# Down products of a four-tile group issued between the pairs of the next group, part of the low-part work moved to VectorE, squares of the norms moved to ScalarE

## The chip, the cores and the metric

One core of a Trainium2 chip runs one program. The metric is the device time of that program in microseconds, the median of the timed runs. The kernel before was run three times.

## The reference

One hybrid decoder layer over 512 tokens with 16 learned meta tokens in front (528 tokens, model width 1024, float32):

```
h = concat(meta, x)
h = h + 0.5 * swiglu(rmsnorm(h, ffn1_norm), w_gate, w_up, w_down)      # d_ff 2816: FFN 1
h = h + concat(gla(hn), sparse_attention(hn)) @ w_out                  # the mixer
h = h + 0.5 * swiglu(rmsnorm(h, ffn2_norm), w_gate, w_up, w_down)      # FFN 2
out = rmsnorm(h, final_norm)[16:]
```

with `swiglu(h) = (silu(h @ w_gate) * (h @ w_up)) @ w_down`. The change touches the two FFNs and the norms that follow them; the mixer between them keeps its instructions.

## The kernel before

All activations lie transposed, feature on the partitions and tokens along the row: h is 8 tiles of 128 x 528. In FFN 1 a product runs over 2 x 264 tokens; in FFN 2 the meta tokens are dropped, so it is 512 (or 2 x 256).

**Three-term products.** Every float32 operand is split into a high part (a copy rounded to fp32r, made on ScalarE) and a low part (operand minus high part, a subtraction). A product is three matmul streams: high by high, high by low, low by high. For the weights the high part is `hi`, `hi_w`, `hi_s` (ACT, L1814 to L1832), and the low part is `lo`, `lo_pair` (POOL, L1704 to L1719).

**Tiles and groups.** The 22 tiles of 128 hidden features are in `GROUPS = [(0, 4), (4, 6), (10, 6), (16, 6)]`. Group 0 is plain: gate and up product of each tile, then silu and the product. Groups 1 to 3 work on two tiles at once with a seven-product scheme (Strassen-Winograd): one *pair* unit is the gate (or the up) weights of two tiles, and is computed in 7 products of half width, each 4 k-steps x 3 streams = 12 matmuls, 84 in all (`pair`, L2235). Even m is a gate pair, odd m an up pair, and two such iterations give two tiles. A pair needs four sums of weight quarters (`sums`, DVE, L2018 to L2023, four operations of 128x512), and its seven products are combined by seven additions on DVE (L2120 to L2134). The low parts of a pair are four POOL operations, in all seven quarters: w11 and w12 (L1711, 1024 wide), w22 (L1714, 512 wide), s2 and s1, and s3 and s4 (L1719, 1024 wide each). After an up pair, DVE multiplies (L2131, L2138), ACT makes the high part `ah` (L1856) and DVE the low part `al` (L2034).

**Down products.** Once a whole group is through, `down` makes the 8 output tiles d, each over all the tiles of the group (L2203), in a ring of four bank pairs; DVE adds each into h (`add_down`, L2056). So TensorE runs 6 pairs in a row, then 8 down products in a row.

**What orders the work.** There is no planner: each engine has its own program, written out in order, with semaphore counts between them. On VectorE, an iteration of a pair is: sums of the next pair, low part of the tiles before, the additions, the multiplications. `w_split` counts weight low parts, `w_used` counts finished products (which free a place of the weights), `c_add` the additions (which free the PSUM banks of a pair), `h_done` the additions into h. Raw weights come through a ring of four slots (`raw`), loaded by SP in the order of use; a load waits until the low part of the unit four before it is made.

**After an FFN.** While the last group's down products run, DVE does for each d: `add_down` (L2056), the square (L1987), the sum of squares (L1990) and, before the mixer, the low part of the mixer's input (L1996); ACT makes its high part (`prep_hi`, L1842). The mixer's first product waits for these low parts one by one. After FFN 2 ACT scales h instead (L1940).

**Plain group.** DVE makes the x operands of the seven-product scheme beside the plain tiles: xn (L2080), their low parts (L2039), and four sums of quarters `x_sums` (L2045 to L2050), all four between the third and the fourth plain tile.

Of the kernel before, what the change touches and what calls it, by code (L numbers as in the profile page):

```python
# [51 lines left out]
GROUPS = [(0, 4), (4, 6), (10, 6), (16, 6)]  # L52
PLAIN = GROUPS[0][1]
FFN_UNITS = 2 * FT + KT * len(GROUPS)
# [18 lines left out]

HALF_UNIT = UNIT // 2
DOWN_PLACES = [0, 2, 4, 6, 8, 10, 12, 8]
PLACE, Q_END, Q_FREE, WIDTH = {}, {}, {}, {}
PAIR_N, PAIRS_OF = {}, {}


def lay_out():  # L80
    taken, q = [0] * 14, 0

    def put(u, place, size, units, width=UNIT):
        nonlocal q
        free, q = max(taken[place:place + size]), q + size
        taken[place:place + size] = [q] * size
        for v in range(u, u + units):
            PLACE[v], Q_END[v], Q_FREE[v], WIDTH[v] = place, q, free, width

    def put_ffn(u, base):  # L90
        for g, (f0, cnt) in enumerate(GROUPS):
            if g == 0:
                for v in range(u, u + 2 * cnt):
                    put(v, 2 * ((v - base) % RING), 2, 1)
            else:
                for n in range(cnt):
                    PAIR_N[u + 2 * n] = len(PAIR_N)
                    put(u + 2 * n, 7 * (n % 2), 7, 2)
            u += 2 * cnt
            for d in range(KT):  # L100
                put(u + d, DOWN_PLACES[d], 2, 1, cnt * P)
            u += KT

    put_ffn(U_FFN1, U_FFN1)
    for u in range(U_MIX, U_FFN2):
        put(u, 2 * ((u - U_MIX) % RING), 2, 1)
    put_ffn(U_FFN2, U_MIX)


lay_out()  # L110

# [6 lines left out]

# [55 lines left out]
def build(nc, x, meta, ffn1, ffn2, mix_norm, w_in, w_a2, b_a, head_norm, w_out, final_norm,  # L174
          cos_t, sin_t, out):
    ctx = ExitStack()
    with ctx:
# [46 lines left out]
        wxh = sb("wxh", [P, 3, UNIT], F32R, ffn_scope)  # L224
        wx_scope = ExitStack()
        wxl = sb("wxl", [P, 3, UNIT], F32R, wx_scope)
        wx_scope.close()
        wxs = sb("wxs", [P, 3, UNIT], F32, ffn_scope)
# [82 lines left out]
        def seven_bank(g, m, i):  # L311

            return (2 * (g - 1) + 7 * m + i) % 8

        def down_bank(g, d):
            return 2 * ((d + g) % 4)
# [3 lines left out]
        w_split = sem("w_split")  # L320
# [643 lines left out]
        def act_mixer(act, hi, prep_hi, root):  # L964
            def keep_part(bank, dst, u, parts):
                ((_, t, n),) = parts
                act.wait_ge(w_used, Q_END[u])
                act.activation(dst[:, t:t + n], ps[:, bank, 0:n], ACT.Copy).then_inc(pj_kept, 1)

            def keep(bank, dst, rows, u, i=None):  # L970
                act.wait_ge(w_used, Q_END[u])
                act.activation(halves(dst), ps[0:rows, bank:bank + 2, 0:HALF], ACT.Copy).then_inc(pj_kept, 1)

            def keep_v(dst, m0, blocks, cols, first):

                act.wait_ge(w_used, Q_END[U_MIX + m0 + 3])
# [213 lines left out]
        def dve_mixer(dve, prep, prep_lo):  # L1190
# [34 lines left out]
            dve.wait_ge(w_used, Q_END[U_MIX + M_IKW])  # L1225
# [22 lines left out]
            dve.wait_ge(w_used, Q_END[U_MIX + M_GV + 3])  # L1248
# [104 lines left out]
            def keep_fill(m):  # L1353

                unit = M_GQK + m
                dve.wait_ge(w_used, Q_END[U_MIX + unit])
# [141 lines left out]
            def add_early(d):  # L1498
                dve.wait_ge(w_used, Q_END[U_OUT + (d - 4) // 2])
# [48 lines left out]
            def add_out(d):  # L1548
                if d % 2 == 0:
                    dve.wait_ge(out_even, d // 2 + 1)  # L1550
                else:
                    dve.wait_ge(w_used, Q_END[U_OUT + 4 + d // 2])
# [24 lines left out]
        def _(sp):  # L1577
            def load(u, src, dst_view):

                slot = u % RING  # L1580
                if u >= RING:
                    sp.wait_ge(w_split, Q_END[u - RING])
                sp.dma_start(dst_view(raw[:, slot, :]), src).then_inc(w_in_slot[slot], 16)
# [19 lines left out]
            def ffn_loads(weights, u0):  # L1603
# [4 lines left out]
                u = u0  # L1608
                for g, (f0, cnt) in enumerate(GROUPS):
                    tiles = range(f0, f0 + cnt)  # L1610
                    if g == 0:
                        order = [(v, f) for f in tiles for v in (gate_v, up_v)]
                    else:
                        order = [(v, f + j) for f in tiles[::2] for v in (gate_v, up_v) for j in range(2)]
                    for v, f in order:
                        load(u, v[:, :, f * P:(f + 1) * P], cols())
                        u += 1
                    for d in range(KT):
                        load(u, down_v[:, f0:f0 + cnt, d * P:(d + 1) * P],
                             lambda s: s[:, 0:cnt * P].rearrange("p (k n) -> p k n", k=cnt))  # L1620
                        u += 1

            ffn_loads(ffn1, U_FFN1)
# [60 lines left out]
            ffn_loads(ffn2, U_FFN2)  # L1684
# [9 lines left out]
        def _(pool):  # L1694
# [6 lines left out]
            def lo(u):  # L1701
                n = WIDTH[u]
                pool.wait_ge(w_hi, Q_END[u])
                pool.tensor_tensor(places(1, PLACE[u], 2)[:, 0:n], raw[:, u % RING, 0:n],  # L1704
                                   places(0, PLACE[u], 2)[:, 0:n].bitcast(F32), ALU.subtract).then_inc(w_split, 2)

            def lo_pair(u):

                at_p, q = operand_places(u), Q_END[u] - 7
# [3 lines left out]
                pool.wait_ge(w_hi, q + 3)  # L1713
                pool.tensor_tensor(places(1, at_p["w22"], 1), raw[:, (u + 1) % RING, HALF_UNIT:UNIT],  # L1714
                                   places(0, at_p["w22"], 1).bitcast(F32), ALU.subtract).then_inc(w_split, 1)
                pool.wait_ge(s_done, 4 * (PAIR_N[u] + 1))
                for n, name in enumerate(("s2", "s3")):
                    pool.wait_ge(w_hi, q + 5 + 2 * n)
                    pool.tensor_tensor(places(1, at_p[name], 2), places(2, at_p[name], 2), places(0, at_p[name], 2).bitcast(F32),  # L1719
                                       ALU.subtract).then_inc(w_split, 2)  # L1720

            def ffn(u, first):

                for g, (_, cnt) in enumerate(GROUPS):
# [44 lines left out]
            ffn(U_FFN1, 1 + len(LEVELS))  # L1769
# [32 lines left out]
            ffn(U_FFN2, 0)  # L1802
# [3 lines left out]
        def _(act):  # L1806
            def hi(u):
                slot, n = u % RING, WIDTH[u]
# [5 lines left out]
                act.activation(places(0, PLACE[u], 2)[:, 0:n], raw[:, slot, 0:n], ACT.Copy).then_inc(w_hi, 2)  # L1814
# [34 lines left out]
            def ffn(u0, number, norm):  # L1849
# [29 lines left out]
                act.wait_ge(w_used, Q_END[u - 1])  # L1879
# [509 lines left out]
```

## Time and profile before

| what | us |
|---|---|
| median of 3 runs | 1109.05 (1108.9 to 1109.67) |
| profiled execution, its own time | 1111.36 |
| its span, first to last instruction | 1109.6 |
| TensorE busy | 1051.8 (95%) |
| VectorE busy | 831.0 (75%) |
| GpSimd (POOL) busy | 635.4 (57%) |
| ScalarE busy | 452.6 (41%) |
| mean granted TensorE clock | 0.99 |

The span is 1.76 us shorter than the execution's own time. Busy shares are means over stages with different limits: in the pair stages three engines are nearly full at once, in the mixer they are not.

### The profile page before, as it was taken

What the parts mean: (1) busy time and instruction counts of PE and PEld (TensorE: products, weight loads), DVE (VectorE), ACT (ScalarE), POOL (GpSimd) and SP (SyncE); (2) the same over time, 40 slices, a digit from 0 to 9 for tenths busy, and PEclk for the clock granted to TensorE, in tenths of its full rate; (3) what the DMA queues carried; (4) which work ended last, traced back from release to release, by engine and by line L of the source; (5) the groups of instructions that cost most, each with busy time, mean ns of one, the idle gap of its engine ahead of it and who ended that gap; (6) DMA issues with size and microseconds to landing.
All of it is one profiled execution on the core that took longest, in us unless ns stands there. A gap on an engine that the chain in (4) does not pass through costs nothing.

```text
span 1109.6 us, 18931 instructions
## 1 busy us (share of the span) xinstructions
PE 1051.8 (95%) x7399; PEld 944.3 (85%) x7399; DVE 831.0 (75%) x1210; ACT 452.6 (41%) x688; POOL 635.4 (57%) x329
## 2 busy tenths in 40 slices
PE   6989999999998999999999999999998999899897
PEld 5989989989998998789767777877888899889886
DVE  5889974895499678699776595578898389649955
ACT  5444342443244344462355516433344234414433
POOL 3657874887488545069710203333888388758750
PEclk8999999999999999999999999999999999999999
DMA  6123433234232534434311102221422432334231
GB/s 193 58 69 104 110 102 94 76 86 125 71 100 68 143 99 112 106 96 125 93 52 39 58 1 77 77 58 38 131 79 78 133 95 77 101 89 115 67 86 76
DMA packets 171740, 98.65 MB, mean 89 GB/s; under 512 B 6275, under 2 KB 167094, under 8 KB 171654
## 3 DMA queue, kind: packets, MB, share of 16 engines
q1 hardware_dynamic: 171654, 97.47, 31.3%
q8 instruction: 59, 0.97, 0.4%
q14 instruction: 27, 0.22, 0.1%
HBM read 91.18 MB, written 2.10 MB: 84 GB/s over the span
## 4 chain that ended last, share of the span: by engine, by line
PE 62%; DVE 21%; issue 8%; POOL 5%; ACT 3%; DMA 1%; SPq 0%; DVEq 0%; POOLq 0%; ACTq 0%
PE ps L2203 35%; PE ps L2235 12%; PE ps L500 5%; PE ps L514 4%; DVE wxs L2018 3%; DVE ws L2019 3%; DVE wxs L2019 2%; DVE ws L2018 2%; POOL wxl L1719 2%; DVE ws L2021 2%; POOL wl L1704 1%; PE ps L637 1%; PE ps L681 1%; PE ps L660 1%; DVE wxs L2021 1%
## 5 line engine op out<-in xcount | busy, mean ns | idle before, releaser
L1704 POOL TENSOR_TENSOR wl<-raw,wh 128x1024 fp32r<-128x1024 f32 (+2 forms) x85 | 187.8, 2219 | 300.7 <-ACT wh L1814 261.7
L2203 PE MATMUL ps<-xh,wh 128*128 128x264 f32 (+3 forms) x416 | 122.8, 342 | 7.1 <-DVE xl L1996 5.8
L2056 DVE SCALAR_TENSOR_TENSOR h<-ps,h 128x528 f32<-128x528 f32 (+1 forms) x64 | 43.8, 695 | 104.2 <-PE ps L2203 104.1
L2203 PE MATMUL ps<-xl,wh 128*128 128x264 f32 (+3 forms) x416 | 117.8, 330 | 0.0
L2203 PE MATMUL ps<-xh,wl 128*128 128x264 f32 (+3 forms) x416 | 117.4, 330 | 0.0
L1719 POOL TENSOR_TENSOR wxl<-wxs,wxh 128x1024 fp32r<-128x1024 f32 x36 | 92.0, 2575 | 36.2 <-ACT wxh L1832 33.5
L2235 PE MATMUL ps<-xh,wh 128*128 128x264 f32 (+1 forms) x360 | 103.6, 288 | 7.3 <-POOL wl L1719 7.2
L1704 POOL TENSOR_TENSOR wxl<-raw,wxh 128x768 fp32r<-128x768 f32 (+1 forms) x32 | 60.3, 1903 | 83.5 <-ACT wxh L1814 83.5
L1719 POOL TENSOR_TENSOR wl<-ws,wh 128x1024 fp32r<-128x1024 f32 x36 | 91.2, 2555 | 22.8 <-ACT wh L1832 18.7
L2235 PE MATMUL ps<-xl,wh 128*128 128x264 f32 (+1 forms) x360 | 101.7, 282 | 0.0
L2235 PE MATMUL ps<-xh,wl 128*128 128x264 f32 (+1 forms) x360 | 101.5, 282 | 0.0
L1814 ACT ACTIVATE wh<-raw 128x1024 fp32r<-128x1024 f32 (+2 forms) x85 | 79.3, 950 | 47.3 <-issue 18.5
L2203 PEld LDWEIGHTS ps<-xh,wh 128*128 128x128 f32 (+1 forms) x416 | 71.2, 191 | 23.9 <-issue 15.9
L2235 PE MATMUL ps<-xh,wxh 128*128 128x264 f32 (+1 forms) x216 | 63.9, 296 | 21.6 <-POOL wxl L1719 21.5
L2203 PE MATMUL ps<-ah,wh 128*128 128x264 f32 (+1 forms) x264 | 72.1, 327 | 5.5 <-DVE al L2034 2.8
L2235 PEld LDWEIGHTS ps<-xh,wh 128*128 128x128 f32 x360 | 67.7, 188 | 10.4 <-POOL wl L1719 10.4
L2203 PEld LDWEIGHTS ps<-xh,wl 128*128 128x128 f32 (+1 forms) x416 | 71.2, 191 | 6.3
L2203 PEld LDWEIGHTS ps<-xl,wh 128*128 128x128 f32 (+1 forms) x416 | 71.2, 190 | 4.8 <-issue 0.2
L2203 PE MATMUL ps<-ah,wl 128*128 128x264 f32 (+1 forms) x264 | 71.7, 326 | 0.0
L2203 PE MATMUL ps<-al,wh 128*128 128x264 f32 (+1 forms) x264 | 71.5, 325 | 0.0
L2203 PE MATMUL ps<-ah,wxh 128*128 128x264 f32 (+1 forms) x264 | 70.5, 321 | 0.0
L2203 PE MATMUL ps<-ah,wxl 128*128 128x264 f32 (+1 forms) x264 | 70.5, 321 | 0.0
(292 smaller groups left out, 3223.7 us busy)
## 6 DMA issues: line engine op xcount, KB each, us to landing
raw<-in_ffn_w_gate SPq DMA_DIRECT2D x44, 512.0 KB, 4.2
raw<-in_ffn_w_up SPq DMA_DIRECT2D x44, 512.0 KB, 4.1
raw<-in_ffn_w_down SPq DMA_DIRECT2D x48, 384.0 KB, 3.9
raw<-in_w_in SPq DMA_DIRECT2D x28, 512.0 KB, 4.0
raw<-in_ffn_w_down SPq DMA_DIRECT2D x16, 256.0 KB, 2.8
raw<-in_w_out SPq DMA_DIRECT2D x8, 512.0 KB, 3.4
xin<-in_x SPq DMA_DIRECT2D x4, 512.0 KB, 4.8
out<-xin SPq DMA_DIRECT2D x4, 512.0 KB, 3.6
```

The lines of the kernel that those rows point to most:

```text
L500: mm = pe.matmul(ps[0:n, V_BANKS[m0][b], :], xx[:, 2 * q + k, s:s + n], ww[:, slot, k * 512:(k + 1) * 512], start=(q == 0 and k == 0 and c ...
L514: return pe.matmul(ps[:, bank, :], ww[:, slot, k * 256 + dd * P:k * 256 + (dd + 1) * P], rr[:, tile, META:TOK], start=(starts and k == 0 a ...
L637: pe.matmul(ps[0:w, qk_bank(n), 0:main_keys(b)], pjb[e:e + HD, pair, s:s + w], pjb[e:e + HD, 4 + pair, 0:main_keys(b)], start=True, stop=T ...
L1704: pool.tensor_tensor(places(1, PLACE[u], 2)[:, 0:n], raw[:, u % RING, 0:n], places(0, PLACE[u], 2)[:, 0:n].bitcast(F32), ALU.subtract).the ...
L1719: pool.tensor_tensor(places(1, at_p[name], 2), places(2, at_p[name], 2), places(0, at_p[name], 2).bitcast(F32), ALU.subtract).then_inc(w_s ...
L1814: act.activation(places(0, PLACE[u], 2)[:, 0:n], raw[:, slot, 0:n], ACT.Copy).then_inc(w_hi, 2)
L2018: dve.tensor_tensor(s1, w21, w22, ALU.add).then_inc(s_done, 1)
L2019: dve.tensor_tensor(s3, w11, w21, ALU.subtract).then_inc(s_done, 1)
L2021: dve.tensor_tensor(s2, s1, w11, ALU.subtract).then_inc(s_done, 1)
L2056: dve.scalar_tensor_tensor(out=as_parts(h[:, d, tk], norm), in0=psum_parts(bank, norm), scalar=0.5, in1=as_parts(h[:, d, tk], norm), op0=A ...
L2203: mm = pe.matmul(ps[0:m, bank + a, 0:width], places(lo, PLACE[u], 2)[:, k * P:k * P + m], r[:, tile, t:t + width], start=(k == first and n ...
L2235: mm = pe.matmul(ps[:, seven_bank(g, m, i), 0:w], places(lo, at_p[wn], 1)[:, k * P:(k + 1) * P], x_operand(xlo, xn, w)[:, k, :], start=(k ...
```

## The change

Four edits, in both FFNs.

1. Groups are now 4 plain tiles, 2, and four times 4. Down products of group g are no longer a stage of their own. They run inside the pairs of group g+1: in each pair, one down product after its third product and one after its seventh. Group 0's down products still run in a row, and so do the last group's. There are six groups of down products instead of four (so 48 additions into h in each FFN instead of 32), over the same 22 tiles: TensorE's matmuls are the same in number and size. A pair uses banks 0 to 5, the down products between use banks 6 and 7 only, so each waits for the addition of the one before. Weight places go from 14 to 16 half units; down weights of four tiles take one place.
2. The low parts of w22 and of s3 and s4 (three of seven) go from POOL to VectorE (`low_pair`), which makes them for the next pair between its second and third addition.
3. After an FFN, ACT squares h (`square`) behind `prep_hi`, and DVE only adds the squares up.
4. Two of the four `x_sums` move behind the fourth plain tile.

```diff
-GROUPS = [(0, 4), (4, 6), (10, 6), (16, 6)]
+GROUPS = [(0, 4), (4, 2), (6, 4), (10, 4), (14, 4), (18, 4)]
+A_TILE = [0, 4, 0, 4, 0, 4]
...
+            def low_pair(u):
+                at_p, n, q = operand_places(u), PAIR_N[u], Q_HI[u] - 7
+                dve.wait_ge(w_hi, q + 3)
+                dve.tensor_tensor(places(1, at_p["w22"], 1), raw[:, (u + 1) % RING, HALF_UNIT:UNIT],
+                                  places(0, at_p["w22"], 1).bitcast(F32), ALU.subtract).then_inc(w_split_dve, 1)
+                dve.wait_ge(w_hi, q + 7)
+                dve.wait_ge(s_done, 4 * (n + 1))
+                dve.tensor_tensor(places(1, at_p["s3"], 2), places(2, at_p["s3"], 2), places(0, at_p["s3"], 2).bitcast(F32),
+                                  ALU.subtract).then_inc(w_split_dve, 2)
...
                     # VectorE, one iteration (g, m); "after" is the next pair
+                    if after:
+                        sums(U_PAIR[(number, *after)])
+                    dve.wait_ge(p1_kept, n + 1)
+                    ...two additions...
+                    if after:
+                        low_pair(U_PAIR[(number, *after)])
+                    if g > 1:
+                        add_down(g - 1, 2 * m)
+                    ...the other additions, and after an up pair the multiplications and low()...
+                    if g > 1:
+                        add_down(g - 1, 2 * m + 1)
+                for d in range(KT):
+                    add_down(last, d)
+                    prep(norm + 1, d)
+                    if number == 0:
+                        prep_lo(norm + 1, d)
...
                     # TensorE
+                def step_down(g, d):
+                    v = U_DOWN[number, g, d]
+                    pe.wait_ge(w_split, Q_END[v])
+                    pe.wait_ge(h_done, hd + KT * g + d)
+                    down(v, 6, order[g], norm, 0, GROUPS[g][1], ft + GROUPS[g][0] if d == 0 else None)
...
+                        for i, (wn, xn_) in enumerate(SEVEN):
+                            if i == DOWN_AFTER and g > 1:
+                                step_down(g - 1, 2 * m)
+                            if i < 2:
+                                pe.wait_ge(w_split, Q_END[v] - 4 + 2 * (i + 1))
+                            elif i == 2:
+                                pe.wait_ge(w_split_dve, 3 * (n + 1))
...
+                        if g > 1:
+                            step_down(g - 1, 2 * m + 1)
...
                     # ScalarE, after an FFN
+                    square(norm + 1, d, hd + d)
...
                     # SP: a load into a slot that held a pair's weights
+                for v in (u - RING, u - RING - 1):
+                    if v in PAIR_N:
+                        sp.wait_ge(w_split_dve, 3 * PAIR_N[v] + 1)
```

## Rows read from the trace of the kernel before

**Rows 1.** The page: busy time of each engine, share, instructions

```profile
PE 1051.8 (95%) x7399; PEld 944.3 (85%) x7399; DVE 831.0 (75%) x1210; ACT 452.6 (41%) x688; POOL 635.4 (57%) x329
```

**Rows 2.** TensorE's waits: waiter, releaser, total us, times, longest

```profile
PE ps L2235 <- POOL wxl L1719: 21.5, 26, 1.1
PE ps L2235 <- POOL wl L1719: 7.2, 9, 1.1
PE ps L2203 <- DVE al L2034: 2.8, 1, 2.8
...
PE ps L2203 <- POOL wl L1704: 2.7, 1, 2.7
```

**Rows 3.** Windows: length, busy us (count) of PE, PEld, DVE, ACT, POOL; clock, DMA, GB/s

```profile
97.80:165.61 67.81, 62.61 (x501) 60.98 (x500) 60.87 (x71) 27.58 (x40) 56.26 (x24) 1.00 0.36 99
165.61:200.67 35.06, 35.06 (x291) 35.06 (x290) 14.74 (x15) 8.46 (x11) 18.48 (x9) 1.00 0.29 82
200.67:267.35 66.68, 62.55 (x507) 61.48 (x506) 58.12 (x71) 28.27 (x40) 53.68 (x23) 1.00 0.36 100
...
898.45:964.76 66.31, 61.57 (x505) 60.15 (x505) 57.96 (x71) 28.09 (x40) 54.10 (x24) 1.00 0.36 100
```

**Rows 4.** Chain that ended last: start us, us, what, matmuls

```profile
302.41 32.04 PE ps L2235 x264
...
369.05 39.43 PE ps L2203 x312
...
772.73 24.09 PE ps L2203 x96
...
865.02 33.43 PE ps L2203 x144
898.45 9.98 PE ps L2235 x84
```

**Rows 5.** Timeline of VectorE: start us, us, operation [idle before]

```profile
67.79 1.24 DVE L2045 TENSOR_TENSOR xn<-xn 128x1056 f32<-128x1056 f32 x1
...
88.27 0.67 DVE L2018 TENSOR_TENSOR ws<-raw 128x512 f32<-128x512 f32 x1
88.87 0.68 DVE L2019 TENSOR_TENSOR ws<-raw 128x512 f32<-128x512 f32 x1
...
100.43 2.88 DVE L2019 TENSOR_TENSOR wxs<-raw 128x512 f32<-128x512 f32 x1
...
106.10 0.43 DVE L2122 TENSOR_TENSOR t<-ps,t 128x264 f32<-128x264 f32 x1
106.45 0.42 DVE L2123 TENSOR_TENSOR t<-ps,t 128x264 f32<-128x264 f32 x1
```

**Rows 6.** Timeline of POOL: the second and last with VectorE out of its way

```profile
99.92 2.84 POOL L1711 TENSOR_TENSOR wxl<-raw,wxh 128x1024 fp32r<-128x1024 f32 x1
...
76.04 2.54 POOL L1704 TENSOR_TENSOR wl<-raw,wh 128x512 fp32r<-128x512 f32 x2 [10.46 <-ACT wh L1814]
...
410.12 2.39 POOL L1704 TENSOR_TENSOR wl<-raw,wh 128x1024 fp32r<-128x1024 f32 x1 [0.86 <-ACT wh L1814]
```

**Rows 7.** Timeline after FFN 1: VectorE's cycle of one d, and ScalarE

```profile
381.07 0.69 DVE L2056 SCALAR_TENSOR_TENSOR h<-ps,h 128x528 f32<-128x528 f32 x1
381.80 0.71 DVE L1987 TENSOR_TENSOR t<-h 128x528 f32<-128x528 f32 x1
382.54 0.71 DVE L1990 TENSOR_TENSOR ss<-ss,t 128x528 f32<-128x528 f32 x1
383.17 0.76 DVE L1996 SCALAR_TENSOR_TENSOR xl<-h,vecs,xh 128x528 fp32r<-128x528 f32 x1
...
401.15 1.05 ACT L1814 ACTIVATE wh<-raw 128x1024 fp32r<-128x1024 f32 x1
404.89 0.74 ACT L1842 ACTIVATE xh<-h,vecs 128x528 fp32r<-128x528 f32 x1 [2.70 <-DVE h L2056]
```

**Rows 8.** Squares on ScalarE at the start, a table load, the clock after a stall

```profile
29.31 0.65 ACT L1961 ACTIVATE t<-h 128x528 f32<-128x528 f32 x1 [0.20 <-DVE ss L2172]
...
31.87 1.28 ACT L1847 ACT_TABLE_LOAD   x1
...
74.00:80.00 6.00, 3.75 (x22) 3.75 (x23) 3.98 (x4) 5.26 (x8) 3.51 (x3) 0.81 0.17 50
```

More of the change, by code:

```diff
@@ new lines, in ffn @@
+                for d in range(3, KT - 1):
+                    hi(U_DOWN[number, last, d])
+                for d in range(KT):
+                    if d == 1:
+                        hi(U_DOWN[number, last, KT - 1])
+                    if number == 0:
+                        if d >= 6:
+                            hi(U_MIX + d - 6)
+                        prep_hi(1, d, hd + d)
+                    square(norm + 1, d, hd + d)
+                    if number:
+                        act.activation(h[:, d, tk], h[:, d, tk], ACT.Copy, scale=gains[:, 3, d:d + 1]).then_inc(y_done, 1)
@@ L1945, in _, with square @@
+            def square(norm, d, h_count):
+                act.wait_ge(h_done, h_count + 1)
+                if d >= 2:
+                    act.wait_ge(ss_done, norm * KT + d - 1)
+                tk = tokens_of(norm)
+                act.activation(t01[:, d % 2, tk], h[:, d, tk], ACT.Square).then_inc(sq_done, 1)
             act.wait_ge(scrap_done, 1)
@@ L2085, in ffn @@
                             x_low(name)
[L2086 to L2087 removed]
+                        x_sums(True)
+                x_sums(False)
                 x_low("t2")
@@ L2155, in _ @@
+                for d in range(KT):
+                    add_down(last, d)
+                    prep(norm + 1, d)
+                    if number == 0:
+                        prep_lo(norm + 1, d)
             for n in range(0, 10, 2):
@@ new lines, in ffn @@
+                for k0, k1, ds in ((0, PLAIN - 1, range(2)), (PLAIN - 1, PLAIN, range(2)), (0, PLAIN, range(2, KT))):
+                    for d in ds:
+                        v = U_DOWN[number, 0, d]
+                        if k0 == 0:
+                            pe.wait_ge(w_split, Q_END[v])
+                            if d < 4:
+                                pe.wait_ge(up_scaled, PLAIN * (number + 1) - 1 + d // 2)
+                            else:
+                                pe.wait_ge(h_done, hd + d - 3)
+                        down(v, down_bank(0, d), tiles, norm, k0, k1, ft if d == 0 else None)
@@ new lines, in ffn @@
+                cnt = GROUPS[last][1]
+                for k0, k1, ds in ((0, 2, range(3)), (2, cnt, range(3)), (0, cnt, range(3, KT))):
+                    for d in ds:
+                        v = U_DOWN[number, last, d]
+                        if k0 == 0:
+                            pe.wait_ge(w_split, Q_END[v])
+                            if 1 <= d < 4:
+                                pe.wait_ge(c_add, 7 * (n + 1))
+                            else:
+                                pe.wait_ge(h_done, hd + KT * last + (d - 3 if d else 0))
+                        down(v, down_bank(last, d), order[last], norm, k0, k1, ft + GROUPS[last][0] if d == 0 else None)
```

495 lines of the change are left out of this document (222 added, 273 removed).

## The prediction

> **What bounds the kernel now.** I read the page's engine shares first: TensorE is busy 1051.8 of 1109.6 us [rows 1], so at most 58 us can be won without removing matmuls, and the change removes none. Then TensorE's own waits: 35 waits for POOL in the pairs, 28.7 us together, each about 1.1 us, and two single waits of 2.8 and 2.7 us around the plain group [rows 2]. Then windows cut at the stage borders, to see where it waits: the down stage of 165.61 to 200.67 is full (35.06 of 35.06 us), with POOL at 18.48 and VectorE at 14.74; the pair stages are not, and there POOL (54 to 56 us of 67) and VectorE (58 to 61 us) are nearly full [rows 3]. So the kernel alternates a stage in which the helpers are the limit with one in which they idle.
>
> How much the pair stages lose: 264 matmuls took 32.04 us, so a pair of 84 takes 10.2 us in FFN 1, and 9.98 us in FFN 2 [rows 4]. Six are 61.2 and 59.9. FFN 1: the first stage starts at the end of the down products, about 97.0, and ends at 165.61, 68.6 us; the other two last 66.7. Lost: 7.4 + 5.5 + 5.4 = 18.3. FFN 2: from 796.8 (772.73 + 24.09) to 865.02 is 68.2, then twice 66.3 [rows 3, 4]: 8.3 + 6.4 + 6.4 = 21.1. Together 39.4 us, and this is what the change can reach, plus the two single waits.
>
> **Why the helpers are slow.** A 128x512 operation of VectorE with both inputs in SBUF starts 0.60 us after the one before when POOL rests, and takes 2.88 us when POOL works; operations that read PSUM keep 0.43 us, 0.35 apart, beside a busy POOL [rows 5]. POOL's 1024-wide operation takes 2.39 us alone and 2.84 against VectorE, the 512-wide one 1.27 alone [rows 6]. The 2.88 us look like one POOL operation plus the own time.
>
> The Trainium skill (SBUF — State Buffer, Who interferes with whom) says that the two engines share a port pair, which one instruction holds whole while the other blocks. By that, each POOL operation delays at most one VectorE operation, by POOL's own duration; the trace agrees (0.60 + 2.39 is close to 2.88). Read as a rate instead, VectorE would run at a quarter of its speed for POOL's 8.7 us of a pair: 8.7 + (5.5 - 2.2) + 3.75 = 15.8 us against the lock's 16.6, both worked out from the terms of the next part. The lock speaks against the change: the low parts moved to VectorE are two more operations that can each be held.
>
> **Part 1 and 2, the steady pairs (groups 3 to 5, 12 pairs in each FFN).** TensorE needs 10.2 + 2 x 24 matmuls at 35.06/288 = 0.122, so 10.2 + 5.8 = 16.0 us for a pair [rows 3, 4]; in FFN 2 9.98 + 2 x 2.79 (33.43/12) = 15.6. POOL per pair: two 1024-wide and two 512-wide, 2 x 2.39 + 2 x 1.27 = 7.3 us: far from full. VectorE alone: sums 4 x 0.60, low parts 0.60 + 1.17, on average one multiplication 0.7 and one `al` 0.65, in all 5.5 us in SBUF; seven additions at 0.35 and two `add_down` at 0.65, 3.75 us from PSUM [rows 5, 7]: 9.3 us. If every POOL operation delays it in full: 9.3 + 7.3 = 16.6. So both engines fit into TensorE's 16 us on average, VectorE just so at worst, and POOL no longer ends last. What is late next is the second down product: it waits for `add_down` of the first, which VectorE does behind sums, two additions and `low_pair`. TensorE asks for it 13.1 us into the pair (3 products 4.4, down 2.9, 4 products 5.8). VectorE starts its iteration 0.7 us in (behind the last `add_down`), sums 2.4 to 6.1, additions 0.7, low parts 1.8 to 5.4, `add_down` 0.65: done between 6.3 and 13.6 us. After an up pair it starts later by the multiplications, the wait for ACT's high part and `al`, some 2 us: up to 15.6. The stall is so 0 to 0.5 us in every other pair and 0 to 2.5 in the rest; I take 0.33 per pair, nearer the low end because POOL's operations are seldom all in the way: 4 us in each FFN (0 to 18).
>
> **Group 2 (4 pairs).** Its downs belong to the group of two tiles, so TensorE has 10.2 + 2.9 = 13.1 us per pair while VectorE still has 9.3 alone, 15.6 with POOL in the way, and about 1.4 of waits for the last down and for ACT. I take 1.25 us per pair, between 0 and 3.9: 5 us in each FFN. **Group 1 (2 pairs, no downs):** the first is made ready beside the plain downs. The first `al` of it is wanted 4.4 us into the next pair: 1 us (0 to 3). Together the pair stages lose 10 us in each FFN, 20 in all, against 39.4.
>
> The new queue order on SP, POOL and ACT I cost at nothing: loads of a pair now wait for VectorE's w22 part, about 10 us into an iteration, and land some 4 to 5 us later, before the sums of the next iteration at 16.7; in group 2 that cover is 13 us, and up to 1 us per pair is in the upper bound above.
>
> **Part 3, behind FFN 1.** Before, VectorE's cycle for one d is 0.73 + 0.74 + 0.63 + 0.68 = 2.8 us under six-tile downs of 4.38 [rows 3, 7]. Now downs take 2.92, and VectorE must wait for ACT: `add_down` 0.73, `prep_hi` 0.65 (its distance to a next operation), square 0.65 and two hand-overs of 0.04 [rows 7, 8], sum 0.63, low part 0.68: 3.4 us. The chain of eight is then longer than TensorE's. From the end of the last pair: down of the group before 2.9, its `add_down` (the last down row begins in its banks) 0.8, two tiles of three downs 4.4, the first finished at 9.6; eight cycles end at 9.6 + 27.4 = 37, and POOL's interference adds about 1. The mixer's first product needs the last low part and ends at 38.5. Without waits it would be 2.9 + 23.4 + 4.4 = 30.7 (before, 39.43 for both with no stall [rows 4]). Loss 8 us (5 to 10). At a stall of 2.8 us the clock was granted at 0.81 in the 6 us around it [rows 8]; two such stalls here, so 1.5 us more. 9.5 in all. Should Square need another table behind Silu, a load of 1.28 us comes on top [rows 8]; squares ran without one at the start, I take 0. Behind FFN 2 the cycle is 0.7 + 0.7 + 0.65 = 2.1 us under 2.79: hidden, and the end of the chain stays the same (a square on ACT for one on VectorE). Only the bank wait stays, 1 us.
>
> **Part 4 and the places, plain group.** The wait for `al` (2.8) goes since two `x_sums` (2.4 us [rows 5]) are out of the way, the wait for `wl` (2.7) since the first down no longer needs a place of the last plain unit. But the same VectorE work then delays the fifth and sixth down, which want its `add_down`: I estimate that 1.3 of 2.8 and 2.2 of 2.7 remain as a gain, 3.5 us (0 to 6).
>
> **Sum.** -39.4 + 20 + 9.5 + 1 - 3.5 = -12.4. Against the profiled execution, 1111.4 - 12.4 = 1099.0; that ran 2.3 us above the median, so 1096.7, and I say 1096.
>
> **Rivals.** (a) *The helpers are fully covered.* For it: both averages lie under 16 us. Pair stages lose 3 us in each FFN and the tail 7: -39.4 + 6 + 8 - 3.5 = -29, 1080. Against it: the single pair of banks for downs. Chance 0.2. (b) *VectorE becomes the bound, slower than before.* Its place is `add_down` behind sums and `low_pair` in one in-order queue. It has 16.6 us at worst against 16.0, and 15.6 against 13.1. It decides once the pairs of groups 2 to 5 lose 1 us each on average (32 pairs: 32 us). At 1.5 us: 50 + 10.5 - 39.4 - 3.5 = +18, 1127. Chance 0.12. (c) *Given back.* The pairs win as forecast, but the chain behind FFN 1 and the plain group cost 10 us more than I say (a table load, a lower clock, late loads): 1106. Chance 0.13. Forecast: 0.55, its own range 1088 to 1104.
>
> **Range and chances.** 1079 to 1112. A change under 0.2% (2.2 us) can't be told from none. Faster 0.8, same 0.07, slower 0.13.
>
> **What would show it.** TensorE's waits for POOL in the pairs are gone; waits for VectorE's h (second down) or its low parts stand there, under 0.5 us per pair in groups 3 to 5 and about 1 in group 2. POOL is well under 60% busy in the pair stages, VectorE over 80%. Between the last pair of FFN 1 and the mixer TensorE waits 6 to 9 us for xl. I am wrong if the steady pairs come out at 17 us or more, or if the tail does not stall.

## The result, and the profile after

| kernel | median us | runs | ratio to before, 95% interval |
|---|---|---|---|
| before | 1109.17 | 1108.9 to 1109.67 | 1 |
| after | 1126.88 | 1126.08 to 1128.01 | 1.016 [1.0142, 1.0177] |

The change costs 17.7 us. The forecast was 1096, and the time lies outside its range; rival (b) gave 1127. The profiled execution of after took 1126.08 (span 1124.4), 0.8 below its median, that of before 1111.36, 2.2 above, so the traces differ by 14.8 us in span.

The page of after answers to [rows 1]:

```profile
PE 1054.5 (94%) x7399; PEld 949.0 (84%) x7399; DVE 922.0 (82%) x1298; ACT 461.3 (41%) x736; POOL 503.3 (45%) x289
```

POOL has lost 132 us of busy time, VectorE has gained 91, and TensorE has the same 7399 matmuls. TensorE's waits, in the columns of [rows 2]:

```profile
PE ps L2253 <- DVE h L2108: 31.9, 26, 4.4
PE ps L2253 <- issue: 8.0, 3, 6.4
...
PE ps L2253 <- DVE xl L2034: 4.1, 1, 4.1
PE ps L2253 <- POOL wxl L1749: 3.6, 2, 1.9
PE ps L2253 <- DVE al L2083: 2.3, 3, 1.0
```

The 35 waits for POOL in the pairs are gone, as said. In their place stand 26 waits of a down product (L2253) for the addition of the one before it (L2108), 31.9 us in all; 23 of them, 28.7 us, lie in the pairs of groups 2 to 5, the other three in the plain groups' down products. The same by stage, in the columns of [rows 3]: FFN 1's group 1, group 2, groups 3 to 5; FFN 2's group 2 and groups 3 to 5; and six microseconds behind one stall:

```profile
95.02:116.45 21.43, 20.61 (x170) 20.43 (x169) 21.29 (x25) 8.05 (x12) 10.03 (x4) 1.00 0.22 62
116.45:180.54 64.09, 56.02 (x435) 55.29 (x434) 60.68 (x73) 22.87 (x36) 30.47 (x18) 0.95 0.38 102
180.54:381.62 201.08, 196.25 (x1586) 194.37 (x1584) 179.91 (x203) 72.93 (x110) 97.30 (x49) 0.99 0.34 92
827.86:891.98 64.12, 54.17 (x387) 51.00 (x385) 60.68 (x74) 22.96 (x37) 30.83 (x18) 0.96 0.39 105
891.98:1089.05 197.07, 189.46 (x1297) 174.64 (x1295) 178.11 (x201) 71.85 (x110) 97.27 (x48) 1.00 0.34 92
133.40:139.40 6.00, 6.00 (x27) 6.00 (x28) 4.53 (x8) 2.88 (x6) 2.15 (x2) 0.51 0.63 170
```

In group 2 and in groups 3 to 5 POOL is busy for half of the time and VectorE for 95% and 90%; TensorE waits while VectorE still has idle time. How that comes about is in one iteration of VectorE in FFN 2 (timeline, the columns of [rows 5]):

```profile
959.73 0.68 DVE L2108 SCALAR_TENSOR_TENSOR h<-ps,h 128x512 f32<-128x512 f32 x1
960.33 1.20 DVE L2056 TENSOR_TENSOR wxs<-raw 128x512 f32<-128x512 f32 x1
961.46 2.88 DVE L2057 TENSOR_TENSOR wxs<-raw 128x512 f32<-128x512 f32 x1
...
966.37 2.84 DVE L2067 TENSOR_TENSOR wl<-raw,wh 128x512 fp32r<-128x512 f32 x1
969.14 2.31 DVE L2071 TENSOR_TENSOR wxl<-wxs,wxh 128x1024 fp32r<-128x1024 f32 x1
971.37 0.68 DVE L2108 SCALAR_TENSOR_TENSOR h<-ps,h 128x512 f32<-128x512 f32 x1
...
975.26 0.69 DVE L2108 SCALAR_TENSOR_TENSOR h<-ps,h 128x512 f32<-128x512 f32 x1 [1.56 <-PE ps L2253]
```

POOL in the same stretch:

```profile
959.69 1.30 POOL L1749 TENSOR_TENSOR wxl<-raw,wxh 128x512 fp32r<-128x512 f32 x1 [6.06 <-ACT wxh L1857]
960.95 2.84 POOL L1756 TENSOR_TENSOR wxl<-raw,wxh 128x1024 fp32r<-128x1024 f32 x1
...
966.26 2.41 POOL L1761 TENSOR_TENSOR wxl<-wxs,wxh 128x1024 fp32r<-128x1024 f32 x1 [2.47 <-ACT wxh L1875]
968.63 1.74 POOL L1749 TENSOR_TENSOR wxl<-raw,wxh 128x512 fp32r<-128x512 f32 x1
```

And TensorE's down product that waits for it, and one in group 2 of FFN 1:

```profile
972.20 0.47 PE L2253 MATMUL ps<-ah,wxh 128*128 128x512 f32 x1 [0.98 <-DVE h L2108]
...
133.40 0.78 PE L2253 MATMUL ps<-ah,wxh 128*128 128x264 f32 x2 [4.22 <-DVE h L2108]
```

The additions of two successive down products stand at 959.73 and 971.37, 11.6 us apart. Four POOL operations ran between, and each held one VectorE operation: 1.20, 2.88, 2.84 and 2.31 us for operations that take 0.60, 0.60, 0.60 and 1.17 alone. TensorE had waited 0.98 us. Then VectorE, through with its additions, idles 1.56 us for the down product that it had made late itself. TensorE waits for VectorE and VectorE for TensorE by turns, so neither is full: one period of two pairs takes 32.87 us (from 958.3 to 991.2 in TensorE's timeline) where TensorE needs 31.1.

The 2.88 and 2.84 us are again near 0.60 plus a whole POOL operation of 2.39 [rows 6]. By the Trainium skill (SBUF — State Buffer, Who interferes with whom) one instruction holds the port pair of the two engines whole; the trace agrees.

### The profile page after: what moved, and what is told of

Same layout as the page of the kernel before. It is cut to its first block and busy times, and to the rows that moved or that the text cites. A ratio compares the mean times of both kernels' runs of the same rounds, so it can differ in the third digit from the quotient of the medians.

```text
span 1124.4 us, 19157 instructions
## 1 busy us (share of the span) xinstructions
PE 1054.5 (94%) x7399; PEld 949.0 (84%) x7399; DVE 922.0 (82%) x1298; ACT 461.3 (41%) x736; POOL 503.3 (45%) x289
## 5 line engine op out<-in xcount | busy, mean ns | idle before, releaser
L1749 POOL TENSOR_TENSOR wl<-raw,wh 128x1024 fp32r<-128x1024 f32 (+1 forms) x65 | 147.5, 2281 | 270.1 <-ACT wh L1857 232.2
L1749 POOL TENSOR_TENSOR wxl<-raw,wxh 128x512 fp32r<-128x512 f32 (+1 forms) x84 | 128.4, 1532 | 223.9 <-ACT wxh L1857 223.9
L2253 PE MATMUL ps<-ah,wxh 128*128 128x264 f32 (+1 forms) x456 | 126.4, 332 | 37.8 <-DVE h L2108 31.9
L2253 PE MATMUL ps<-xh,wh 128*128 128x264 f32 (+3 forms) x416 | 123.3, 343 | 12.3 <-issue 6.4
L2253 PE MATMUL ps<-ah,wxl 128*128 128x264 f32 (+1 forms) x456 | 124.0, 327 | 0.0
L2253 PE MATMUL ps<-al,wxh 128*128 128x264 f32 (+1 forms) x456 | 123.6, 326 | 0.0
L2253 PEld LDWEIGHTS ps<-ah,wxh 128*128 128x128 f32 x456 | 77.2, 193 | 50.4 <-issue 39.8
L2253 PE MATMUL ps<-xl,wh 128*128 128x264 f32 (+3 forms) x416 | 118.2, 331 | 0.0
L2253 PE MATMUL ps<-xh,wl 128*128 128x264 f32 (+3 forms) x416 | 117.8, 330 | 0.0
L2108 DVE SCALAR_TENSOR_TENSOR h<-ps,h 128x528 f32<-128x528 f32 (+1 forms) x96 | 65.7, 691 | 42.0 <-PE ps L2253 41.8
L2067 DVE TENSOR_TENSOR wl<-raw,wh 128x512 fp32r<-128x512 f32 x36 | 99.5, 2763 | 0.0
L2253 PEld LDWEIGHTS ps<-xh,wh 128*128 128x128 f32 (+1 forms) x416 | 71.4, 191 | 29.3 <-issue 21.3
L2253 PEld LDWEIGHTS ps<-ah,wxl 128*128 128x128 f32 x456 | 77.5, 193 | 6.7
L2253 PEld LDWEIGHTS ps<-al,wxh 128*128 128x128 f32 x456 | 77.4, 192 | 5.2
L2253 PEld LDWEIGHTS ps<-xh,wl 128*128 128x128 f32 (+1 forms) x416 | 71.4, 191 | 6.3
L2253 PEld LDWEIGHTS ps<-xl,wh 128*128 128x128 f32 (+1 forms) x416 | 71.4, 191 | 4.8 <-issue 0.2
L1857 ACT ACTIVATE wh<-raw 128x1024 fp32r<-128x1024 f32 (+1 forms) x65 | 61.5, 971 | 19.4 <-PE ps L536 15.6
```

Source lines behind the costliest of these rows:

```text
L1749: pool.tensor_tensor(places(1, PLACE[u], c)[:, 0:n], raw[:, u % RING, 0:n], places(0, PLACE[u], c)[:, 0:n].bitcast(F32), ALU.subtract).the ...
L1857: act.activation(places(0, PLACE[u], c)[:, 0:n], raw[:, slot, 0:n], ACT.Copy).then_inc(w_hi, c)
L2067: dve.tensor_tensor(places(1, at_p["w22"], 1), raw[:, (u + 1) % RING, HALF_UNIT:UNIT], places(0, at_p["w22"], 1).bitcast(F32), ALU.subtrac ...
L2108: dve.scalar_tensor_tensor(out=as_parts(h[:, d, tk], norm), in0=psum_parts(bank, norm), scalar=0.5, in1=as_parts(h[:, d, tk], norm), op0=A ...
L2253: mm = pe.matmul(ps[0:m, bank + a, 0:width], places(lo, PLACE[u], -(-WIDTH[u] // HALF_UNIT))[:, k * P:k * P + m], r[:, tile, t:t + width], ...
```

## Experiments

All ran beside the kernel before; ratios are to it. Parts 1 to 4 are those of the change. Group 2 and *steady* pairs (groups 3 to 5) are given by the start-to-start distance of pairs, worked out from TensorE's timeline; TensorE needs 16.0 us (FFN 1) and 15.5 to 15.6 (FFN 2) for a steady pair. After has 19.7, 14.5, 15.0, 14.9 in group 2 of FFN 1.

**1. All low parts back on POOL, part 2 undone (e1_low_pool).**

```diff
+                # POOL, in lo_pair
+                pool.wait_ge(w_hi, q + 3)
+                pool.tensor_tensor(...w22...).then_inc(w_split_dve, 1)
+                pool.wait_ge(w_hi, q + 7)
+                pool.tensor_tensor(...s3, s4...).then_inc(w_split_dve, 2)
-                        low_pair(U_PAIR[(number, *after)])
```

> The changed kernel with the three quarters of low parts (w22, s3, s4) back on POOL, everything else as changed. Theory Q (the bound of the pair stages is VectorE's one in-order queue: the second down product waits for add_down, which sits behind sums and low_pair): the 11 to 11.6 us from the start of sums to the first add_down fall by low_pair's 4 to 5, TensorE's waits for h go, the pair stages lose 10 to 15 us of TensorE instead of 47: 1127 falls to about 1093. Rival P (POOL becomes the limit again, with 9.7 us of work alone in a pair of 16, 11.7 held by VectorE): 1105 or more, with waits for POOL's low parts as before.

Measured 1106.94, ratio 0.9977 [0.9968, 0.9987]. Steady pairs took 16.02 in FFN 1 and 15.52 in FFN 2, what TensorE needs, except the first of each (19.9 and 20.3). Part 2 costs 20 us on top of part 1 as it is placed, although POOL is the busier without it. Rival P's time came, but not its waits: TensorE waited once for POOL in the pairs, 1.0 us. What is missing from the 1093 expected is in group 2 (59.8 against 52.5 in FFN 1, 56.7 against 51.1 in FFN 2) and in those two first pairs. In group 2 VectorE waits for raw weights, for 16.8 of these 21.3 us:

```profile
DVE ws L2061 <- DMA raw<-in_ffn_w_gate: 21.3, 8, 4.8
```

In after the same wait is 2.7 us in 3 times. Experiments 8 and 9 look into it.

**2. The square back on VectorE, part 3 undone (e2_sq_dve).**

```diff
-                    square(norm + 1, d, hd + d)
+                dve.tensor_tensor(t1[:, tk], h[:, d, tk], h[:, d, tk], ALU.mult).then_inc(sq_done, 1)
```

> The changed kernel with the squares after both FFNs back on VectorE. Theory: behind FFN 1 the cycle of one d falls from 3.4 us (VectorE waits for prep_hi and the square on ScalarE) to 2.8, eight times, so the stall in front of the mixer (6.65 us in the changed kernel) shrinks by about 4.5 and the half-rate stretch behind it too: 1127 falls to 1121 or 1122. Rival: the stall is made by the short down products alone (2.92 us each), then under 1 us changes.

Measured 1128.46, ratio 1.0163 [1.0146, 1.018]: no gain. Windows of it behind FFN 1 (the gap, and the mixer's first matmuls):

```profile
406.00:412.00 6.00, 2.96 (x18) 2.77 (x17) 5.86 (x7) 3.37 (x4) 3.70 (x2) 0.83 0.04 7
412.00:418.00 6.00, 6.00 (x21) 5.67 (x21) 5.29 (x6) 1.69 (x2) 2.28 (x2) 0.60 0.59 142
```

The same windows of after:

```profile
406.00:412.00 6.00, 0.22 (x2) 0.00 (x0) 3.51 (x6) 3.28 (x5) 2.11 (x1) 0.74 0.00 0
412.00:418.00 6.00, 5.41 (x22) 5.41 (x23) 3.54 (x5) 3.37 (x5) 4.43 (x3) 0.69 0.73 163
```

The gap before the mixer is 3.3 us shorter, but the matmuls behind it run at half rate for about 6 us instead of 3.3 (a step of 0.33 us instead of 0.18), which takes back 1.5. The other 1.8 are a gain in this place: from the last down product to the mixer's matmuls at full rate it is 10.5 us (407.61 to 418.07) against 12.3 (406.22 to 418.50). The rest of the kernel doesn't keep it. This execution came to the gap 1.4 us later; it loses 1.1 in the mixer, where a stall of 1.9 us that after has too is followed by half the clock, and 2.0 in FFN 2. Its granted clock over the span is 0.980, that of after 0.984.

**3. The first `add_down` ahead of `low_pair` (e3_add_first).** The same work on every engine, one swap in VectorE's program.

```diff
-                    if after:
-                        low_pair(U_PAIR[(number, *after)])
                     if g > 1:
                         add_down(g - 1, 2 * m)
+                    if after:
+                        low_pair(U_PAIR[(number, *after)])
```

> The changed kernel with one line of VectorE moved: the first add_down of a pair comes before low_pair, not behind it. The work of each engine is the same. Theory Q (order in the queue): TensorE no longer waits for h at the second down product; stalls of 1.8 to 4.4 us in group 2 and their stretches at half clock go, about 0.8 us per pair in groups 3 to 5 goes in part, since VectorE's work of 31.3 us per two pairs (32.87 less 1.56 idle) then is the bound: 1105 to 1112. Rival W (VectorE's amount of work is the limit, whatever its order): 1124 to 1130.

Measured 1104.4 (1102.32 to 1108.07), ratio 0.9962 [0.9948, 0.9975]: 22.5 us under after. Steady pairs 16.02 and 15.52, the first of each 18.0 and 16.9. Its waits, which answer to the 31.9 us above:

```profile
PE ps L2253 <- DVE h L2108: 9.9, 7, 2.8
```

and an iteration of VectorE in the same stretch of FFN 2:

```profile
951.25 0.68 DVE L2108 SCALAR_TENSOR_TENSOR h<-ps,h 128x512 f32<-128x512 f32 x1
951.85 2.24 DVE L2067 TENSOR_TENSOR wl<-raw,wh 128x512 fp32r<-128x512 f32 x1
954.01 2.31 DVE L2071 TENSOR_TENSOR wxl<-wxs,wxh 128x1024 fp32r<-128x1024 f32 x1
...
957.90 0.68 DVE L2108 SCALAR_TENSOR_TENSOR h<-ps,h 128x512 f32<-128x512 f32 x1
960.29 0.99 DVE L2056 TENSOR_TENSOR ws<-raw 128x512 f32<-128x512 f32 x1 [1.71 <-issue]
```

In this iteration the low parts are held much as before (2.24 and 2.31), but nobody waits for them, and VectorE idles 1.71 us before the next sums. The number and size of VectorE's operations are unchanged, so they weren't the limit; their order was. The holds didn't stay quite the same, though: VectorE is busy for 897.5 us instead of 922.0, and most of that is w22's low part, first in after, then here (count, busy us, mean ns):

```profile
L2067 DVE TENSOR_TENSOR wl<-raw,wh 128x512 fp32r<-128x512 f32 x36 | 99.5, 2763 | 0.0
L2067 DVE TENSOR_TENSOR wl<-raw,wh 128x512 fp32r<-128x512 f32 x36 | 81.3, 2257 | 0.0
```

How the 22.5 us divide between the place of `add_down` and these shorter holds was not tested. Group 2 still took 59.2 us in FFN 1 (14.1, 14.2, 17.7, 13.1) and 59.6 in FFN 2.

**4. Only part 2, on the kernel before (b2_low_dve).**

```diff
-                # POOL: w22, s3 and s4
+                    # VectorE, in the pair behind the second addition
+                        if m < cnt - 1:
+                            low_pair(v + 2)
```

> The kernel before, with only the three quarters of low parts moved from POOL to VectorE (its groups of 6 and its down stages stay). By Q and W alike VectorE, already at 58 to 61 of 67 us in the pair stages, ends last: in the changed kernel the two pairs of group 1, which have no downs, took 8.9 and 13.4 us of VectorE, 11.1 on average against TensorE's 10.2 and 11.1 before: 1109 plus or minus 5. If POOL alone had been the limit before, waits of 28.7 us would go: 1085.

Measured 1093.26, ratio 0.9854 [0.9837, 0.987]. I had expected 1109: a miss by 16 us. Its waits:

```profile
PE ps L2253 <- DVE wl L2032: 13.0, 6, 2.2
...
PE ps L2253 <- POOL wxl L1718: 1.1, 4, 0.3
```

The 28.7 us for POOL [rows 2] have become 1.1, with 13.0 us in six waits for the last low part of a pair. Without down products between the pairs, no `add_down` stands behind `low_pair`; in the pairs TensorE waits for low parts alone, 14.1 us where it was 28.7. Of the change as it was made, part 2 by itself is the gain; part 1 with it turned −16 into +18 (parts 3 and 4 are worth under 2 us there, experiments 2 and 7). Experiment 10 shows that part 1 is not a loss in itself.

**5. Part 3 alone, on the kernel before (b3_sq_act).**

```diff
-                dve.tensor_tensor(t1[:, tk], h[:, d, tk], h[:, d, tk], ALU.mult).then_inc(sq_done, 1)
+                        square(norm + 1, d, hd + d)
```

> The kernel before with only part 3: squares after both FFNs on ScalarE. Six-tile downs take 4.38 us each, a cycle on VectorE through ScalarE 3.4, before 2.8: both are covered, so 1109 plus or minus 1.5. Rival: the last cycle alone, which nothing covers, gets longer by the hand-over to ScalarE: plus 1 us in FFN 1.

Measured 1108.56, ratio 0.999 [0.9981, 1.0]: nothing. Under down products of six tiles the chain behind an FFN is hidden, as expected.

**6. Only s3 and s4 on VectorE, w22 on POOL, on the kernel before (b4_s3_dve).**

```diff
+                # POOL keeps w22, as a third operation; otherwise as 4
+                pool.tensor_tensor(...w22...).then_inc(w_split, 1)
```

> The kernel before with only the low parts of s3 and s4 on VectorE; w22's stays on POOL. Moving all three won 16 us and left one wait of 2.4 us for VectorE in the fifth pair of each group and a long sixth pair (26.8 to 27.0 us for both, against 20.4). If these come from VectorE being behind by about 1 us a pair, they shrink with 0.6 to 2.8 us less per pair, while POOL has 6.1 us of 10.2: 1093 falls to about 1084. Rival: POOL's third operation holds VectorE as often as VectorE's own cost, then 1093 to 1097.

Measured 1099.9, ratio 0.9913 [0.9897, 0.993]: 6.6 us *over* experiment 4, where I had expected it under.

```profile
PE ps L2250 <- DVE wxl L2029: 9.5, 12, 0.8
PE ps L2250 <- POOL wxl L1718: 9.1, 12, 1.1
PE ps L2250 <- POOL wl L1718: 6.7, 8, 1.0
```

VectorE has 0.6 us less to do per pair and POOL one operation more, and TensorE waits for both. By the two pages, VectorE is busy for 866.0 us here with 1246 operations, and for 860.8 with 1282 in experiment 4: 36 operations fewer, and 5 us more. POOL is busy for 539.3 against 477.7. So what VectorE saves by giving the operation away it loses again by being held by it.

**7. Part 4 undone (e5_xsums_back).**

```diff
                         x_sums(True)
-                x_sums(False)
+                        x_sums(False)
```

> The changed kernel with part 4 undone: all four x_sums between the third and fourth plain tile again. If the split was a gain, a wait of 2 to 3 us for al comes back in front of the first downs of both FFNs: 1127 rises to 1129 to 1131. Rival: the four stalls of 1.0 to 2.3 us (6.5 us with their half-clock stretches) that the changed kernel has in FFN 2's plain downs come from the split, since the two late sums push every low part and add_down back; then it falls to 1124 to 1126.

Measured 1126.64, ratio 1.0157 [1.014, 1.0174]: as after. The waits for `al` are back, 2.5 us in FFN 1's plain group and 3.0 in FFN 2's, but POOL's two of 1.7 and 1.9 are gone there, and others shrink by the rest.

**8. Experiment 3 with w22 on POOL (e6_s3_first).** It tests whether the load of raw weights, which waits for w22's low part, is what is left in group 2.

```diff
+                # POOL makes w22's low part; SP no longer waits for w_split_dve
-                        sp.wait_ge(w_split_dve, 3 * PAIR_N[v] + 1)
```

> The changed kernel with the first add_down ahead of the low parts, and w22's low part back on POOL (s3 and s4 stay on VectorE). Theory L: what is left in group 2 once the order is right is a loop through the ring of raw slots (load waits for w22's low part on VectorE, 5.7 us to land, sums, ACT, low part: 14.1 us against TensorE's 13.1); with w22's low part made early on POOL it opens, group 2 loses 2 us instead of 6.7 in each FFN: 1104 falls to about 1096. Rival: VectorE's work in group 2 is the limit there, then only the 0.6 to 2.8 us of the operation itself go: 1101 to 1104.

Measured 1105.72, ratio 0.9968 [0.9955, 0.998]; I had expected 1096, so the link was the wrong one. Group 2 of FFN 1 stays at 15.3, 14.2, 16.7, 13.1. SP's queue in it (start, time, the load):

```profile
117.49 0.99 SPq L1619 DMA_DIRECT2D raw<-in_ffn_w_up  x2
...
131.62 0.99 SPq L1619 DMA_DIRECT2D raw<-in_ffn_w_gate  x2
...
145.86 0.99 SPq L1619 DMA_DIRECT2D raw<-in_ffn_w_up  x2
```

and VectorE's first sum of each iteration:

```profile
123.26 2.33 DVE L2055 TENSOR_TENSOR wxs<-raw 128x512 f32<-128x512 f32 x1 [2.63 <-DMA raw<-in_ffn_w_up]
...
137.47 2.36 DVE L2055 TENSOR_TENSOR ws<-raw 128x512 f32<-128x512 f32 x1 [2.48 <-issue]
```

Loads go out every 14.1 us, a sum starts 5.8 us behind its load, and VectorE had idled 2.5 us for it. That is a loop: load, sums, ACT's high part, POOL's low part of s2, next load. It takes 14.1 us, and TensorE needs 13.1 in group 2. The load waits for *all* of `w_split` of the pair, which s2's low part ends; but s2 is made from the sums, no longer from the raw slot.

**9. The load freed as soon as the raw weights are read (e7_early_load).** Experiment 8, and:

```diff
-                if u >= RING:
+                if pair_of:
+                    sp.wait_ge(w_split, Q_END[pair_of[0]] - 2)
+                    sp.wait_ge(s_done, 4 * (PAIR_N[pair_of[0]] + 1))
+                elif u >= RING:
                     sp.wait_ge(w_split, Q_END[u - RING])
```

> e6 (first add_down ahead of the low parts, w22 on POOL) with one more edit on SP: the load of a pair's weights no longer waits for s2's low part, which reads other memory, but for what reads the slot: the sums and the low parts of w11, w12 and w22. In e6 group 2 keeps 13.9 to 16.7 us per pair, and its loads are issued every 14.1 us, 3.7 us after the sums are over. Theory R (the loop is load 5.8 us, sums 5.3, ACT, POOL's low part): it falls to about 11 us, under TensorE's 13.1; group 2 loses 2 us instead of 6.8 in each FFN, and VectorE's waits for raw go: 1106 falls to 1096 to 1098. Rival: something else holds group 2 (VectorE being late from group 1), then 1103 to 1106.

Measured 1093.53, ratio 0.986 [0.9844, 0.9877]: 12.2 us from one wait. Group 2 is now 13.9, 13.1, 14.1, 13.1. This confirms that the release of the raw slot was the link.

**10. Experiment 3 with w22's low part right behind the sums, and the early load (e8_w22_after_sums).** All three low parts on VectorE.

```diff
                     if after:
                         sums(U_PAIR[(number, *after)])
+                        low_w22(U_PAIR[(number, *after)])
                     ...two additions, add_down...
                         low_pair(U_PAIR[(number, *after)])    # now s3 and s4 alone
```

> As e7, but all three low parts on VectorE as in the change: w22's right behind the sums (so that its slot comes free), then two additions, add_down, then s3 and s4. On the kernel before, w22 on VectorE was better than on POOL by 6.6 us (1093.3 against 1099.9). If that holds between downs too, 1 to 4 us under e7. Rival: in pairs of 16 us both engines are off the path and it makes no difference.

Measured 1087.18 (1086.85 to 1087.34), ratio 0.9802 [0.9786, 0.9819]: under both kernels, and 6.3 under experiment 9. Waits, then windows of group 2 and of groups 3 to 5 in FFN 1:

```profile
PE ps L2261 <- issue: 8.0, 3, 6.3
...
PE ps L2261 <- DVE h L2114: 4.7, 6, 1.4
```

```profile
116.63:170.27 53.64, 53.10 (x434) 52.57 (x433) 52.65 (x72) 22.62 (x36) 32.49 (x17) 1.00 0.40 113
170.27:362.60 192.33, 192.33 (x1586) 192.25 (x1584) 160.50 (x204) 74.01 (x110) 105.28 (x50) 1.00 0.34 96
```

Group 2 takes 53.6 us where after took 64.1, groups 3 to 5 take 192.3 where after took 201.1, with TensorE busy in all but 0.5 us of it and the clock at 1.00. VectorE's busy time in groups 3 to 5 is 160.5 against 179.9 for the same work. Its w22 low part is hardly held any more in its new place, 0.89 us against 2.76:

```profile
L2069 DVE TENSOR_TENSOR wl<-raw,wh 128x512 fp32r<-128x512 f32 x36 | 32.1, 893 | 0.2
```

Of what the traces of 9 and 10 differ by (6.1 us), 3.1 lie ahead of group 2, in the plain groups and group 1, and 3.3 in groups 2 to 5; so the pairs gained within the 1 to 4 us expected, and the rest was not foreseen. Against experiment 4 this kernel is 6.1 us faster: parts 1, 3 and 4 together with the order and the earlier load. Experiment 4 with an earlier load was not run; the list of VectorE's waits there has none for raw weights.

**11. Experiment 4 with part 4 and another weight place for group 0's first down (b5_low_dve_plus).**

```diff
-                        x_sums()
+                        x_sums(True)
+                x_sums(False)
```

> The kernel before with part 2 (low parts on VectorE), part 4 (x_sums split) and the first plain down product in a place that is free (the place part of the change). Part 2 alone gave 1093.3, with one stall of 2.6 us for al in FFN 1 and one of 3.0 us for the weights' low part in front of FFN 2's downs. If both go without coming back, 1088 to 1090; by the runs of the change, where the plain stage came out no shorter, about 1092.

Measured 1093.57, ratio 0.9861 [0.9845, 0.9878]: no gain over 4. The waits of the plain group move (FFN 2 has two, of 1.9 and 2.0 us, elsewhere) and don't go.

**12. Experiment 10 without part 3 (e9_sq_dve).** The edit of 2 on the kernel of 10.

> e8 with part 3 undone: squares after both FFNs on VectorE. In e2, on the changed kernel, this cut the stall in front of the mixer from 6.65 to 3.3 us, but the half-clock stretch behind it grew from 3.3 to 6 us and the time did not fall. Theory: the stall is worth its length, so e8's 6.6 us shrink to about 3.3 and 1087 falls to 1084. Rival: the clock takes it back as in e2, 1086 to 1088.

Measured 1085.5 (1083.21 to 1086.22), ratio 0.9776 [0.9763, 0.979]: the fastest of all, though its interval just meets that of 10. The stall before the mixer came in three pieces, 3.0, 0.5 and 2.0 us, and the clock held:

```profile
380.00:392.00 12.00, 8.96 (x71) 8.77 (x70) 11.72 (x15) 4.85 (x6) 3.73 (x2) 1.00 0.03 6
392.00:398.00 6.00, 3.53 (x18) 2.86 (x17) 5.30 (x6) 1.68 (x2) 2.28 (x2) 1.00 0.57 141
```

Up to there the profiled execution gained 2.4 us on that of experiment 10; 1.3 of them went in the mixer, where the stretch at half the clock from 644.8 is 6.9 us long instead of 3.4.

## Why the prediction was wrong

By its own steps, in us of the profiled executions (measured: start-to-start distances of pairs less TensorE's need, so with the half clock behind a stall in them):

| step | forecast | measured |
|---|---|---|
| pair stages of before | −39.4 | −39.4 |
| group 1, both FFNs | 2 | 2.2 |
| group 2, both FFNs | 10 | 11.6 + 13.0 = 24.6 |
| groups 3 to 5, both FFNs | 8 | 8.6 + 10.3 = 18.9 |
| tail behind FFN 1 | 9.5 | 9.2 |
| bank wait behind FFN 2 | 1 | 1.1 |
| plain groups | −3.5 | −1.9 + 1.5 = −0.4 |
| mixer | 0 | −1.6 |
| sum | −12.4 | 14.6 (spans: 14.8) |

**The step that failed is Part 1 and 2 with group 2:** the stall of the second down product, taken as 0.33 us per steady pair and 1.25 in group 2. The loss was 0.7 and 0.9 per steady pair (FFN 1 and 2; in FFN 1 3.5 of the 8.6 us in the first of them), and about 3 in group 2. The mechanism was named (`add_down` behind sums and `low_pair`, held by POOL), with `add_down` done between 6.3 and 13.6 us into the pair, up to 15.6 after an up pair. I took the low end, "because POOL's operations are seldom all in the way". The trace shows all four in the way, in the steady loop as a rule: POOL's operations start when ACT's high parts of the same weights are ready, which is when VectorE works on their sums and low parts. w22's low part alone averages 2.76 us over its 36, against 0.60. The two engines are in step, not at random. Experiment 3 settles that the order decided 22.5 us: the same operations, with nothing of TensorE's behind the held ones. It also made the holds shorter. Rival (b) had the right place, and its time is what came; its chance of 0.12 was too small. That its number came to within 0.1 us is luck: it had 50 us in the pair stages and −3.5 in the plain groups, where 45.7 and −0.4 came, and nothing in the mixer. Nor was it right that VectorE is the bound by its work: 16.6 against 16.0 us was its reason, and experiments 3 and 10 do the same work in 16.0. Rival (b)'s threshold (1 us on average over the 32 pairs) was passed at (24.6 + 18.9)/32 = 1.4. The sign "steady pairs at 17 us or more" did not show: they came at 16.8 and 16.4 on average. It left group 2 out, where more than half of the loss was. (The 15.8 us of the reading as a rate took 8.7 us for POOL, where the terms beside it have 7.3, which would make it 14.7; nothing of the sum hung on it.)

**Loads at nothing.** "The new queue order on SP, POOL and ACT I cost at nothing" failed in group 2. With the order of experiment 3, 6.7 and 8.5 us (FFN 1 and 2) of the 11.6 and 13.0 are still lost there, in experiment 8 6.8 and 6.1, and with the earlier load of 9 1.7 and 2.5. The loop from load to load is 14.1 us, longer than the 13.1 that TensorE needs there, and freeing the raw slot one step earlier is worth 12 us (8 against 9). My guess that w22's part was the link was wrong too; it was s2's. In before a down stage stands between the groups of pairs; that this gave the loads time to catch up is my reading, not shown.

**What the clock added.** A stall of 4.2 us at 133.40 was followed by six microseconds at a granted clock of 0.51, at a matmul step of 0.22 us instead of 0.12. By the granted clock, TensorE was busy at half the clock for 15.9 us from the plain group of FFN 1 to the mixer's first matmuls, and for 6.9 in FFN 2, in before for 3.4 in each. Half of such time is lost: 8.0 and 3.5 us against 1.7 and 1.7; they are inside the terms above.

**What held.** Waits for POOL went. Group 1 and the bank wait came as said. The chain behind FFN 1 did: the last cycle but one of VectorE there,

```profile
396.60 0.70 DVE L2108 SCALAR_TENSOR_TENSOR h<-ps,h 128x528 f32<-128x528 f32 x1
398.69 0.71 DVE L2028 TENSOR_TENSOR ss<-ss,t 128x528 f32<-128x528 f32 x1 [1.40 <-issue]
399.32 0.76 DVE L2034 SCALAR_TENSOR_TENSOR xl<-h,vecs,xh 128x528 fp32r<-128x528 f32 x1
400.00 0.70 DVE L2108 SCALAR_TENSOR_TENSOR h<-ps,h 128x528 f32<-128x528 f32 x1
```

is 3.4 us with 1.40 of waiting for ACT's square, and TensorE's first matmul of the mixer answers with

```profile
412.59 0.67 PE L2253 MATMUL ps<-xh,wh 128*128 128x400 f32 x1 [6.37 <-issue]
```

within the 6 to 9 us given. The plain groups did not hold: each removed stall came back nearby, in FFN 2 in full (waits of 0.6, 1.9, 1.0, 1.4 and 1.0), and experiments 7 and 11 show part 4 to be worth nothing.

**What stays open.** Why stalls of 1.7 and 2.0 us in after (ending at 80.7, 195.8 and 889.7) were followed by half the clock, and ones of 1.9 and 2.6 (ending at 792.6 and 874.8) by the full one, was not tested. Nor was the part of the early load in experiment 10 taken alone, nor why the plain groups are slower with w22's low part on POOL (9 against 10). Whether 12 beats 10 is within the intervals.

## What to carry to other kernels

When work of one engine is moved behind another's in an in-order queue, ask first which operation of that queue a third engine waits for, and put that one ahead of everything with slack: the sum of busy times (9.3 + 7.3 against 16) said that it fits, and the order decided 22 us. Where two engines hold each other up and both follow the same event, take the high end for the operations between, not an average. And follow each ring of buffers as a loop: time from one load to the next through everything that frees the slot, against the shortest stage, since 14.1 against 13.1 us cost 12 us that no engine's busy share showed; VectorE's waits for raw weights did.

## What the runs showed of the hardware

- A hold by POOL can cost VectorE more than the operation that it spares it: one 512-wide subtraction moved from POOL to VectorE in every pair gave 6.6 us (1099.9 to 1093.26), and VectorE, with 36 operations more, was busy for 5 us less (860.8 against 866.0).
- How long VectorE is held depends on where the operation stands: w22's low part took 2.76, 2.26 and 0.89 us on average in three places of VectorE's program (after, 3, 10), 0.60 alone.
- A shorter stall isn't worth its length: in experiment 2 it was 3.3 us shorter, and the slow-clock stretch behind it grew from 3.3 to 6 us, which took back 1.5. Split into three shorter stalls (12) it left the clock at 1.00.
- A load of raw weights takes 5.8 us from its issue to the first sum in group 2 (117.49 to 123.26 in experiment 8), against a median of 4.1 from issue to landing over after; in group 2 the DMA moves 102 to 105 GB/s, 92 in groups 3 to 5.
- Squares on ScalarE behind FFN 1 came without a table load in after: the doubt of Part 3 was void.
